# A hybrid trunk layer in fp32: the gated rows of the scan move into its units, and the second half of the conditioning product into the units of the neighbourhood attention

## What is computed

```python
mod = jax.nn.silu(c) @ ada_w[l] + ada_b[l]           # c_ctx for the context rows: 6 vectors of 1024
sh1, sc1, g1, sh2, sc2, g2 = jnp.split(mod, 6, axis=-1)
h = rmsnorm(x, norm1_g) * (1 + sc1) + sh1            # then one projection h @ w_in
m_out = mlstm(...)                                   # 4 heads, two directions
y = scan(...)                                        # Mamba-2 scan, 6 heads, two directions
s_out = rmsnorm(y * silu(z), s_norm_g)               # the mean is over the 384 columns of a row
a_out = neighbourhood_attention(...)                 # 6 heads, 8 x 16 window on a 16 x 64 grid
x = x + g1 * (concat([m_out, s_out, a_out]) @ w_out)
h2 = rmsnorm(x, norm2_g) * (1 + sc2) + sh2
x = x + g2 * expert_choice_moe(h2)                   # 16 experts, each takes its top rows
```

## Time and profile before

| | us |
|---|---|
| median of 3 runs (lowest, highest) | 1820.76 (1820.05, 1821.52) |
| the profiled execution, its own time | 1817.82 |
| its span, first to last instruction | 1816.1 |
| PE busy | 1675.5 (92%) |
| DVE / ACT / POOL busy | 739.0 / 383.0 / 426.6 |
| chain that ended last | PE 86%, DVE 5%, DMA 4%, ACT 2% |

### The profile page before, as it was taken

One profiled execution on the slowest core, in us unless ns is written; L12 is line 12 of the kernel. 1 busy time (PEld: TensorE's weight loads), 2 busy tenths in 40 slices (PEclk: granted clock), 3 DMA queues, 4 the chain that ended last, 5 costly groups with the idle time before them and its releaser, 6 DMA issues.

```text
span 1816.1 us, 29608 instructions
## 1 busy us (share of the span) xinstructions
PE 1675.5 (92%) x11761; PEld 1463.5 (81%) x11761; DVE 739.0 (41%) x1837; ACT 383.0 (21%) x903; POOL 426.6 (23%) x496
## 2 busy tenths in 40 slices
PE   5999999979999288889999999999999999999991
PEld 3967877746678166579889999999999999999991
DVE  3001165667555398112253343443332343443333
ACT  5111123331211266101111111111111111111112
POOL 2000000034322343011112332222223333232223
PEclk9999999989999599889999999999999999999996
DMA  9311100021110650932338988888888888888836
GB/s 325 112 55 38 30 20 24 24 84 42 35 36 27 140 136 1 320 119 97 104 140 297 337 270 268 302 297 274 292 278 267 282 284 271 285 295 289 290 84 233
DMA packets 203710, 322.46 MB, mean 178 GB/s; under 512 B 30064, under 2 KB 91353, under 8 KB 203643
## 3 DMA queue, kind: packets, MB, share of 16 engines
q1 hardware_dynamic: 179227, 283.18, 44.7%
q0 software_dynamic: 10160, 19.62, 5.4%
q10 hardware_dynamic: 14256, 18.75, 3.1%
HBM read 290.77 MB, written 27.54 MB: 175 GB/s over the span
## 4 chain that ended last, share of the span: by engine, by line
PE 86%; DVE 5%; DMA 4%; ACT 2%; issue 1%; SPq 1%; POOL 1%; ACTq 0%; POOLq 0%; DVEq 0%
PE psum L1649 28%; PE psum L1664 14%; PE psum L1280 13%; PE psum L1283 9%; PE psum L1544 7%; PE psum L1414 1%; PE psum L1200 1%; DVE gt L2019 1%; DVE gt L2031 1%; PE psum L1560 1%; PE psum L1324 1%; PE psum L1675 1%; DMA arena<-in_ada_w 1%; PE psum L1623 1%; PE psum L1535 1%
## 5 line engine op out<-in xcount | busy, mean ns | idle before, releaser
L1649 PE MATMUL psum<-arena 128*128 128x144 f32 x4096 | 504.8, 286 | 2.5 <-DVE arena L2205 2.4
L1649 PEld LDWEIGHTS psum<-arena 128*128 128x128 f32 x4096 | 502.8, 190 | 3.0 <-DVEq L2213 2.5
L787 POOL DMA_INDIRECT expert_list<-gt x136 | 151.8, 1116 | 455.5 <-DVE gt L2236 380.2
L1664 PE MATMUL psum<-arena 128*128 128x144 f32 x2048 | 255.2, 287 | 0.0
L1664 PEld LDWEIGHTS psum<-arena 128*128 128x128 f32 x2048 | 251.7, 190 | 0.4
L1280 PE MATMUL psum<-arena 128*128 128x384 f32 x720 | 243.0, 493 | 0.1
L2251 DVE TENSOR_TENSOR arena<-gt,psum 128x144 f32<-128x144 f32 x128 | 39.0, 304 | 418.7 <-PE psum L1649 393.4
L1280 PEld LDWEIGHTS psum<-arena 128*128 128x128 f32 x720 | 134.3, 191 | 91.1 <-issue 3.5
L2117 DVE SCALAR_TENSOR_TENSOR arena<-arena,gt 128x1024 f32<-128x1024 f32 x136 | 168.9, 1278 | 0.0
L1283 PE MATMUL psum<-arena 128*128 128x256 f32 (+2 forms) x864 | 165.9, 353 | 0.0
L1283 PEld LDWEIGHTS psum<-arena 128*128 128x128 f32 x864 | 146.2, 192 | 18.1 <-issue 1.9
(11 more groups left out here) (338 smaller groups left out, 1808.3 us busy)
## 6 DMA issues: line engine op xcount, KB each, us to landing
arena<-in_exp_w SPq DMA_DIRECT2D x96, 2048.0 KB, 9.7
arena<-in_ada_w SPq DMA_DIRECT2D x24, 1024.0 KB, 8.5
arena<-in_w_in SPq DMA_DIRECT2D x11, 1024.0 KB, 4.9
arena<-affinity_rows SPq DMA_DIRECT2D x17, 512.0 KB
arena<-in_x_sample SPq DMA_DIRECT2D x16, 512.0 KB, 5.1
arena<-decay_rows ACTq DMA_DIRECT2D x24, 192.0 KB, 3.3
out<-arena SPq DMA_DIRECT2D x9, 512.0 KB
arena<-in_w_out SPq DMA_DIRECT2D x4, 1024.0 KB, 8.5
```

The source lines that it names most:

```text
L787: pool.indirect_dma_start(out=list_d, out_offset=bass.IndirectOffsetOnAxis(ap=rank_i[:, c:c + 1].bitcast(U32), axis=0), in_=pair[:, c, :], ...
L1649: ins = mm(bank[:, 0:SLOTS], w[:, k, col], xeT[:, k, :], start=(k == 0), stop=(k == KD - 1))
L1664: ins = mm(bk[4 + db % 2][:, 0:SLOTS], wslot[4 + db // 4][:, k, (db % 4) * P:(db % 4) * P + P], hid[:, k, :], start=(k == 0), stop=(k == K ...
```

## The change

`DONE` lists the nine tiles of the scan with the unit after which each is complete. Stage 4 is done tile by tile: DVE gates a tile at the end of that unit, ACT squares it and DVE makes the mean in the next, POOL takes the power, DVE scales in the one after, and for seven tiles PE turns it as a group "Y" in a slot of `S_FILL`, evacuated by ACT in place. The last two (`LATE`) are turned at the start of the attention. Projection groups go into 33 slots instead of 36. `z` lies in ring slots 2 and 3 and is loaded in unit 11, as are the cached keys and values, and the state is stored there.

The slabs 8 to 23 go into 16 of the 27 attention units (`MOD_UNITS`), all in bank 7; ACT adds the bias. g1 is turned once, written to a small DRAM buffer and read back spread over the partitions. All values go to bank 6. The wait for the router's weights moves to the router. Idle products are fewer.

```diff
+    DONE = [(0, 12), (5, 12), (4, 13), (6, 13), (3, 14), (7, 14), (2, 15), (8, 16), (1, 17)]
+    done_at = {u: [k for k, (_, w) in enumerate(DONE) if w == u] for u in range(2 * NT)}
+    LATE = 2
...
-    S_FILL = spread(n_first, len(groups), 36)
+    base, S_FILL = spread(n_first, len(groups), 33) + [[], [], []], []
+    merged = groups[:n_first]
+    for slot in range(36):
+        k0 = len(merged)
+        merged += [groups[n] for n in base[slot]]
+        if slot == 32:
+            n_proj = len(merged)
+        for k, (ch, u) in enumerate(DONE[:NT - LATE]):
+            if slot == 2 * (u + 2) + 1:
+                merged.append(("Y", None, 0, 384, k, ("mixS", ch), "A"))
+        S_FILL.append(list(range(k0, len(merged))))
+    groups = merged
...
-        mixA = view(R_Y, 3, T)
+        mixA = view(R_S + 3460, 3, T)
...
-        z = view(R_S, NT, 384)
-        mixS = view(R_S + 3460, 3, T)
+        z = view(R_RING + 2 * KD * SLAB, NT, 384)
+        y_junk = view(R_M + 11136, 384)
...
+        MOD_UNITS = [3, 4, 6, 7, 9, 10, 12, 13, 15, 16, 18, 19, 21, 22, 24, 25]
...
-            sp.wait_ge(pj_full, len(pe_groups))
+            sp.wait_ge(pj_full, pe_index[n_proj - 1] + 1)
             for hp in range(2):
                 load_rel(hp)
-            sp.wait_ge(pj_act, evacuated("A", len(groups)))
-            sp.wait_ge(yz, 1)
+            sp.wait_ge(pj_act, evacuated("A", n_proj))
+            sp.wait_ge(yz, NT)
             for hp in range(2):
                 load_values(hp)
-            for m in range(8, 8 + RING):
+            for m in range(8, 18):
                 load_slab(G1 + m - 8)
             sp.wait_ge(tab_done, 6)
             load_rel(2)
+            for m in range(18, 20):
+                load_slab(G1 + m - 8)
             sp.wait_ge(aO, done_with_pair(0))
             load_values(2)
-            for m in range(8, 24):
-                if m >= 8 + RING:
-                    load_slab(G1 + m - 8)
+            for m in range(20, 24):
+                load_slab(G1 + m - 8)
             for j in range(4):
                 load_slab(WOUT + j)
+            sp.wait_ge(aO, done_with_pair(1))
+            sp.wait_ge(g1_moved, 16)
+            for e in range(2):
+                src = bass.AP(tensor=g1_d.tensor, offset=g1_d.offset + e * P, ap=[[0, P], [2 * P, KD], [1, P]])
+                sp.dma_start(g1b[:, e, :].rearrange("p (b n) -> p b n", n=P), src).then_inc(g1_moved, 16)
...
+            def y_rstd(k):
+                ch = DONE[k][0]
+                pool.wait_ge(msq_done, RS_S + k + 1)
+                pool.tensor_tensor(rstd[:, 1, ch:ch + 1], rstd[:, 1, ch:ch + 1], half[:, 0:1], ALU.pow).then_inc(rstd_done, 1)
...
+                if u >= 3:
+                    for k in done_at[u - 3]:
+                        y_rstd(k)
...
+            pool.wait_ge(pj_full, pe_index[n_proj - 1] + 1)
             pool.wait_ge(colmask_in, 16 * (HR - 1))
-            for kind in range(3):
-                make_mask(0, kind)
-            pool.wait_ge(msq_done, RS_S + 1)
-            pool.tensor_tensor(rstd[:, 1, :], rstd[:, 1, :], half[:, 0:NT], ALU.pow).then_inc(rstd_done, 1)
+            make_mask(0, 0)
+            for k in done_at[16]:
+                y_rstd(k)
+            make_mask(0, 1)
+            make_mask(0, 2)
             for i in range(2):
                 pool.memset(tab[:, i, :, 384:512], 0.0)
+            for k in done_at[17]:
+                y_rstd(k)
+            for i in range(2):
+                make_table(i)
             for kind in range(3):
...
+                elif target[0] == "mixS":
+                    for b in range(3):
+                        ins = nc.scalar.activation(yacc[:, target[1], b * P:b * P + P], ps[:, b * P:b * P + P], ACT.Copy,
+                                                   scale=vcol[:, V_SG + b:V_SG + b + 1])
...
+            def y_square(k):
+                act.wait_ge(yz, k + 1)
+                if k >= 1:
+                    act.wait_ge(sumsq_done, SQ_S + k)
+                ch = DONE[k][0]
+                nc.scalar.activation(y_junk, yacc[:, ch], ACT.Square, accum_out=sumsq[:, 1, ch:ch + 1]).then_inc(sumsq_done, 1)
...
+                if u == 11:
+                    act.wait_ge(*last_read[19])
+                    act.dma_start(z, z_d.rearrange("(t p) n -> p t n", p=P)).then_inc(z_in, 16)
+                    act.dma_start(ckT, cacheT_k.rearrange("(b p) t -> p b t", p=P)).then_inc(cache_in, 16)
+                    act.dma_start(cv, cache_v).then_inc(cache_in, 16)
+                    act.wait_ge(out_done, 16 * 18)
+                    act.wait_ge(sH, 2)
+                    for d in range(NDIR):
+                        for g in range(GS):
+                            q = slice(HD * g, HD * g + HD)
+                            act.dma_start(new_sT[d, q, :], Hst[q, d, g, :]).then_inc(out_done, 16)
+                if u >= 1:
+                    for k in done_at[u - 1]:
+                        y_square(k)
...
+            def late_row(m):
+                act.wait_ge(mod_full, m + 1)
+                act.wait_ge(modT_full, m - 1)
+                nc.scalar.activation(mrow[:, m % 2, :], bk[7][:, 0:SLAB], ACT.Copy).then_inc(mrow_full, 1)
+            def late_col(m):
+                act.wait_ge(modT_full, m + 1)
+                for b in range(2):
+                    ins = nc.scalar.activation(modcol[:, 2 * m + b, :], bk[7][:, 256 + 2 * b:258 + 2 * b], ACT.Identity,
+                                               bias=vcol[:, V_ADAB + 2 * m + b:V_ADAB + 2 * m + b + 1])
+                ins.then_inc(modT_done, 1)
...
+                if a - 1 in MOD_UNITS:
+                    late_col(8 + MOD_UNITS.index(a - 1))
                 a_turn(a)
-            for m in range(8, 24):
-                mod_row(m)
+                if a == 0:
+                    y_late(1)
+                if a in MOD_UNITS:
+                    late_row(8 + MOD_UNITS.index(a))
+                if a == MOD_UNITS[3] + 1:
+                    act.wait_ge(g1_full, 1)
+                    nc.scalar.activation(gt[0:16, 24, :], bk[7][0:16, 384:512], ACT.Copy).then_inc(g1_full, 1)
+                    act.wait_ge(g1_full, 2)
+                    act.dma_start(g1_d, gt[0:16, 24, :]).then_inc(g1_moved, 16)
...
-                if a >= 2:
-                    pe.wait_ge(aN, a - 1)
+                if a >= 1:
+                    pe.wait_ge(aN, a)
...
-                        out = bk[6 + a % 2][HD * e:HD * e + HD, 0:P]
+                        out = bk[6][HD * e:HD * e + HD, (a % 2) * P:(a % 2) * P + P]
...
+            def late_product(m):
+                slab_ready(G1 + m - 8)
+                pe.wait_ge(modT_done, m)
+                pe.wait_ge(s_rows_a, LATE)
+                if m == 12:
+                    pe.wait_ge(g1_full, 2)
+                for k in range(KD):
+                    q = k % 4
+                    ins = mm(bk[7][32 * q:32 * q + 32, 0:SLAB], scol32[:, k, :], ring[:, (G1 + m - 8) % RING, k, :],
+                             start=(k < 4), stop=(k >= 4), tile_position=(0, 32 * q))
+                ins.then_inc(mod_full, 1)
+            def late_pick(m):
+                pe.wait_ge(mrow_full, m + 1)
+                for b in range(2):
+                    ins = mm(bk[7][:, 256 + 2 * b:258 + 2 * b], mrow[:, m % 2, b * P:b * P + P], pick[:], start=True, stop=True)
+                ins.then_inc(modT_full, 1)
...
+            pe.wait_ge(sY, NU)
             pe.wait_ge(pj_act, evacuated("A", len(groups)))
             a_scores(0)
             a_scores(1)
+            y_late(0)
             for a in range(NA):
                 if a + 2 < NA:
                     a_scores(a + 2)
                 if a >= 1:
                     a_values(a - 1)
+                if a - 1 in MOD_UNITS:
+                    late_pick(8 + MOD_UNITS.index(a - 1))
                 a_turned(a)
+                if a == 0:
+                    y_late(1)
+                if a in MOD_UNITS:
+                    late_product(8 + MOD_UNITS.index(a))
+                if a == MOD_UNITS[3] + 1:
+                    pe.wait_ge(modT_done, 12)
+                    nc.tensor.transpose(bk[7][0:16, 384:512], modcol[:, 16:24, :].rearrange("p a b -> p (a b)"), ident[:])\
+                        .then_inc(g1_full, 1)
...
+            def y_gated(k):
+                ch = DONE[k][0]
+                dve.wait_ge(z_in, 32)
+                v.tensor_tensor(yacc[:, ch], yacc[:, ch], z[:, ch], ALU.mult).then_inc(yz, 1)
+            def y_mean(k):
+                ch = DONE[k][0]
+                dve.wait_ge(sumsq_done, SQ_S + k + 1)
+                v.tensor_scalar(rstd[:, 1, ch:ch + 1], sumsq[:, 1, ch:ch + 1], 1.0 / 384, EPS, ALU.mult, ALU.add)\
+                    .then_inc(msq_done, 1)
+            def y_scale(k):
+                ch = DONE[k][0]
+                dve.wait_ge(rstd_done, RS_S + k + 1)
+                v.tensor_scalar(yacc[:, ch], yacc[:, ch], rstd[:, 1, ch:ch + 1], None, ALU.mult).then_inc(s_y, 1)
...
```

(72 more changed lines are left out.)

79 lines of the change are left out of this document (28 added, 51 removed).

## The result

| | before | after |
|---|---|---|
| median of 4 runs each (lowest, highest), us | 1820.99 (1820.05, 1821.52) | 1770.10 (1767.41, 1773.37) |
| ratio, 95% interval | | 0.9722 (0.9704 to 0.9739) |
| the profiled execution, its own time | 1817.82 | 1773.37 |
| its span | 1816.1 | 1771.6 |
| PE busy | 1675.5 (92%) | 1660.1 (94%) |

The change makes the kernel 50.9 us faster; 53.6 was forecast. The stretches that answer to the earlier trace rows (the scan is as full as before, 194.6 of 196 us) are the start of the attention and the attention with the products.

A forecast was written before the change was run, and what follows sets the result against it. The prediction took PE, 92% busy, as the bound, with gains where it stands still. Output start 45.8, first tile 2.3 and idle runs 5.5 sum to 53.6 us off 1820.8: 1767.2, 8-in-10 range 1752 to 1790.

The forecast's parts named there:

- the likeliest case: Whole kernel: the stages come out as summed, 1767 us, own range 1756 to 1782, 60% chance.
- Step 1: Attention's start: gated rows moved, SP's queue limits, from 588.3 to first slab at 629.8; unit 3 reached 19.3 us earlier.
- The attention's natural arrival at unit 3: Attention's start: left alone it would reach unit 3 at 616, so the slab at 629.8 decides.
- The wait of unit 1's values: Sign at the attention's start: PE waits for values in unit 1 before the slab's wait; no size given.
- Step 2: Attention: sixteen products add 24.8 us, 14.1 fill PE's waits, new waits 8.5; 19 taken, plus 3 for half clock.
- Rival A: Attention: the clock falls and stays down, adding 95 us less the 3 counted, 1859; 3% chance.
- Rival B: Attention: shared-bank waits cost 2 us, not 0.5, in each of 16 units, +24, 1791; 12% chance.
- Step 3: Behind the attention: output starts at 734.3, 45.8 us earlier; first tile 2.3 less; g1 and router's weights cost nothing.
- Step 4: Ahead of the experts: fewer idle products and earlier sums and gathers; 5.5 us less taken, 3.7 if gathers don't move.
- The experts, about 806 us, stay: Experts' stage, behind the shorter idle runs: its length was forecast unchanged at about 806 us.
- Rival C: Attention: slabs 18 to 23 come late for two or three products, 8 us, 1775; 8% chance.
- Rival D: Attention's start: the queue isn't the limit, up to 13.8 us less, 1754; 10% chance.

The follow-up runs named there:

- e3: The changed kernel with SP's queue reordered, the second head pair's window and value loads behind the slabs needed first: 1753.69 us, ratio 0.9634.
- experiment 2, e4: The changed kernel with each of the sixteen conditioning products done twice: 1783.34 us, ratio 0.9793.
- experiment 4, e1: The kernel before with only the shorter idle runs of the changed one: 1819.25 us, ratio 0.9986.
- experiment 8: The reordered kernel with 13 instead of 9 idle products ahead of the experts, 1754.36 us, beside the reordered kernel run again, 1754.58 us.
- e3_again: The changed kernel with SP's queue reordered, measured a second time: 1754.58 us, ratio 0.9633.
- e5: The changed kernel with the sixteen products left behind the attention, so only the gated rows move, shared edits kept: 1793.60 us, ratio 0.9854.
- e7: The reordered kernel with POOL making the first bias table before the second and third mask: 1761.57 us, ratio 0.9669.
- e9: The reordered kernel with 13 instead of 9 idle products in the last run ahead of the experts: 1754.36 us, ratio 0.9627.

## Why the prediction was right

The forecast was 1767 and the time is 1770.1, inside the range and inside the likeliest case's own.

- **Step 1, the queue.** Right in kind and order. It started at 593.19, not 588.3. 4.8 of the 4.9 come from the scan of this one execution (last section); e3, with the same code up to there, started at 589.26. Window loads 15.95 for 15.4; value loads 21.76 for 20.75; landing 5.4 for 5.3. The product of unit 3 was at 636.53 for 629.8, so 1.9 of the 6.7 belong to the queue. The attention's natural arrival at unit 3 was put at 616; e3 has it at 619.12, its own wait for the first table included. The wait of unit 1's values, which the prediction names among its signs, was 4.46; it needs no term, since unit 3 waits for the slab anyway.
- **Step 2, sixteen products.** From unit 3 to the attention's end it was 82.1 us. It is 98.1 in e3 at full clock: 16.0, where 19 were taken. The cover is real: waits other than the slab's fell from 14.1 to 7.3 (8.5 taken). Half clock behind the slab cost 3.4 (3 taken). Rival A didn't come: the clock is 1.00 from 644 on and 0.96 over the whole stretch. Rival B falls at 2 us a unit: one bank by itself costs 4.4 in 27 units. A change of the tiling mode drains TensorE, as the Trainium skill (TensorEngine Tiling (Array Packing), Tiling Modes) states. Nothing shows beyond the product's own time, as the prediction took it: a product takes 1.01 us to the scores behind it (643.82 to 644.83), for 1.00 to the pick in before. Both rows have a change of mode in them, so they don't give its price; experiment 2 bounds it. A second product straight behind the first, in the same mode, adds 0.86 where a product by itself takes 1.00. An estimate from these: the changes of mode around a product cost at most 0.14 us, 2.2 for all sixteen.
- **Step 3, the output.** It starts 41.7 earlier, 46.5 without the 4.8 of the scan (last section), for 45.8. The first tile takes 14.08 (13.9). The return of g1 through memory and the router's weights cost nothing: PE waits for neither. The later waits ahead of the output, which the step has no term for, were 6.4 us to be had alone.
- **Step 4, idle runs.** This is the term that was off: 5.5 taken, 2.6 measured. The 5.5 themselves came (6.0 in the profile); the sentence "The experts, about 806 us, stay" failed. They are 3.1 us longer in after. The clock is at 0.79 in their first 8 us (the 256 products take 33.7 for 31.75) and the second gather is 0.74 late, which together is 2.7. The experts start at 919.16 for 913.
- **The sum.** The forecast of 1767.2 misses the median by 2.9, and the term of Step 4 is off by 2.9. That the rest comes out even is in part luck: the queue brought unit 3's slab 1.9 later than summed, and the products cost 3.0 less.
- **Rival C**, late slabs in the middle, didn't come: no product but the first waits for a DMA, and so none runs behind the attention. **Rival D** has the right mechanism for e3: take the queue away and 16 us come (13.8 at most were taken).

## What to carry to other kernels

When a stage that idles is filled, look at the queues whose issues it had hidden, and put first the loads that the first unit needs: a pure change of order was worth 16 us here, a third of the whole change. When two parts don't add up, measure the edits that they share by themselves before the difference is explained: here 4.6 of 12.0 us were counted twice, and the rest is no larger than its uncertainty. A stop that the profile puts down to one load can have others landing just ahead of it, so look up when each load that is waited for lands before one wait is moved. Idle work that seems free to remove may be what holds the clock for the stage behind it: 6.0 us were cut and 2.6 stayed (experiment 4), though four products put back did not bring the clock back (experiment 8).

## What the runs showed of the hardware beside that

- The first group of the scan took 6.6 to 6.7 us in 5 of 12 profiles (before, e3, e3_again, e5, e7) and 7.8 to 8.2 in the other 7, in kernels of both kinds. The granted clock from 380 to 400 was 0.70 in before and 0.58 in after. The group began 1.55 us later in after than in before and ended 3.1 later (399.3 for 396.1). A second such place follows only in after, e4 and e9: a group at 461 takes 7.12 us, 5.43 in e3, with a clock of 0.66 from 460 to 465 in after and 1.00 in e3. These three have the gated rows in the scan and the long first group; the four others with the rows and the short first group don't show it, nor do the five without the rows. Why isn't shown. Together after is 4.8 us late against before, and 3.9 against e3, at a place where after and e3 have the same code. So the medians are to be compared, and traces stage by stage. The first group in before, both in after, and the second place in e3:

```profile
389.51 6.60 PE L1280 MATMUL psum<-arena 128*128 128x384 f32 x16
```

```profile
391.06 8.19 PE L1348 MATMUL psum<-arena 128*128 128x384 f32 x16
...
461.05 7.12 PE L1348 MATMUL psum<-arena 128*128 128x384 f32 x16
```

```profile
458.82 5.43 PE L1352 MATMUL psum<-arena 128*128 128x384 f32 x16
```

- The issue of one window load took SP 0.48 us alone (7.71 for 16), 0.50 in after (15.95 for 32), 0.69 beside the loads of `z` (22.20 for 32 in e1), and 0.86 right behind four slabs of 1 MB (13.75 for 16 in e3). So the price of a small load was not one number; that it goes with what else is moving is how these rows lie, and no run tests it.
- The half clock outlasts the stop: in after the granted clock is 0.70 from 600 to 612 and 0.81 to 634. Behind the stop, from 636 to 642, it is 0.50 while PE is busy 5.46 of the 6 us, and from 644 it is 1.00. In e3, without the stop, it is 1.00 from 612. Rows of after, then of e3:

```profile
612.00:634.00 22.00, 11.63 (x84) 8.26 (x82) 11.92 (x26) 8.92 (x21) 10.98 (x13) 0.81 0.42 108
636.00:642.00 6.00, 5.46 (x40) 3.36 (x40) 1.44 (x6) 1.12 (x4) 0.00 (x0) 0.50 1.09 386
644.00:660.00 16.00, 14.87 (x174) 10.61 (x167) 10.69 (x25) 10.07 (x24) 4.30 (x4) 1.00 0.63 209
```

```profile
612.00:634.00 22.00, 20.69 (x230) 15.02 (x232) 18.16 (x47) 15.60 (x37) 11.09 (x12) 1.00 0.95 274
```
